# Gated-delta pairs: scaling inside the inversion, first solve ahead of the sixth output slot, outputs of both directions in one bank

## The reference, cut to what matters

```
u = rms_norm(h);  z = u @ w_in            # one input projection for all three groups
y = concat(rwkv7(z_rw), gated_delta(z_gd), mlstm(z_ml))
h = h + y @ w_out
h = h + (silu(gate) * val) @ w_down       # gate, val from conv(rms_norm(h) @ w_up)
h = h + sigmoid(rms_norm(h) @ w_ple_gate) * (p @ w_ple_proj)
```

```
L   = strict_lower((k * beta) @ k.T * decay)
u,w = solve(I + L, [v * beta, k * beta * exp(g)])
v_new = u - w @ S
o = (q * exp(g)) @ S + lower(q @ k.T * decay) @ v_new
S = S * exp(g_last) + (k * exp(g_last - g)).T @ v_new
```

## Time and profile before

| what | us |
|---|---|
| median of three runs | 3178.64 (3175.67 to 3181.02) |
| the profiled execution, its span | 3174.6 |
| PE busy in it | 3054.9 (96%) |
| DVE busy | 2081.5 (66%) |
| ACT busy | 1657.2 (52%) |
| POOL busy | 612.3 (19%) |

### The profile page before, as it was taken

One profiled execution on the slowest core, in us unless ns is written; L12 is line 12 of the kernel. 1 busy time (PEld: TensorE's weight loads), 2 busy tenths in 40 slices (PEclk: granted clock), 3 DMA queues, 4 the chain that ended last, 5 costly groups with the idle time before them and its releaser, 6 DMA issues.

```text
span 3174.6 us, 56293 instructions
## 1 busy us (share of the span) xinstructions
PE 3054.9 (96%) x20767; PEld 2626.2 (83%) x20767; DVE 2081.5 (66%) x3474; ACT 1657.2 (52%) x2673; POOL 612.3 (19%) x517
## 2 busy tenths in 40 slices
PE   8999988899999999999999999889899999999998
PEld 7899877777888888888788998777688888888886
DVE  6775655777777777455568655567767777774554
ACT  6555654456555555444455556545465555544444
POOL 2000453440212222000000005334402221220000
PEclk9999998999999999999999999999899999999999
DMA  6666101114656666666556660021256665666664
GB/s 208 185 180 187 47 2 59 61 55 146 195 185 192 192 182 196 221 195 191 164 169 194 183 178 15 2 66 55 67 178 193 184 192 181 196 198 215 193 183 152
DMA packets 265227, 479.22 MB, mean 151 GB/s; under 512 B 17314, under 2 KB 81148, under 8 KB 264380
## 3 DMA queue, kind: packets, MB, share of 16 engines
q1 hardware_dynamic: 265020, 476.48, 49.1%
HBM read 474.32 MB, written 2.10 MB: 150 GB/s over the span
## 4 chain that ended last, share of the span: by engine, by line
PE 87%; DVE 8%; ACT 1%; issue 1%; DVEq 1%; POOL 0%; SPq 0%; DMA 0%; ACTq 0%; POOLq 0%
PE ps L643 86%; PE ps L647 1%; DVE scores L2194 1%; DVE wlo L1801 1%; DVE XS L1851 0%; ACT L1272 0%; DVE upair L1814 0%; DVE TN L1860 0%; DVE AR L2221 0%; DVE H L1833 0%; ACT XS L1272 0%; DVE st L1875 0%; DVE TN L2246 0%; DVE heads L1880 0%; POOL H L580 0%
## 5 line engine op out<-in xcount | busy, mean ns | idle before, releaser
L1801 DVE TENSOR_TENSOR wlo<-ring,whi 128x1024 fp32r<-128x1024 f32 (+4 forms) x905 | 1095.6, 1229 | 672.2 <-ACT whi L1272 666.3
L643 PE MATMUL ps<-upair,whi 128*128 128x512 f32 x4032 | 1404.4, 394 | 6.3 <-DVE upair L1814 5.7
L1272 ACT ACTIVATE whi<-ring 128x1024 fp32r<-128x1024 f32 (+4 forms) x947 | 941.0, 1002 | 795.6 <-PE ps L643 715.8
L643 PE MATMUL ps<-upair,wlo 128*128 128x256 f32 x4032 | 1121.2, 278 | 0.0
L643 PEld LDWEIGHTS ps<-upair,whi 128*128 128x128 f32 x4032 | 756.5, 188 | 182.9 <-issue 6.1
L643 PEld LDWEIGHTS ps<-upair,wlo 128*128 128x128 f32 x4032 | 758.9, 188 | 0.3 <-issue 0.2
L643 PE MATMUL ps<-whi,upair 128*128 128x390 f32 (+2 forms) x1280 | 367.5, 364 | 0.0
L625 POOL TENSOR_TENSOR YB<-YB 128x1024 f32<-128x1024 f32 x22 | 125.3, 5697 | 828.9 <-DVE YB L1824 828.9
L643 PE MATMUL ps<-whi,ghi 128*128 128x512 f32 x704 | 274.4, 390 | 0.0
L643 PE MATMUL ps<-whi,glo 128*128 128x512 f32 x704 | 274.0, 389 | 0.0
L643 PE MATMUL ps<-wlo,ghi 128*128 128x512 f32 x704 | 273.9, 389 | 0.0
(11 more groups left out here) (311 smaller groups left out, 3621.5 us busy)
## 6 DMA issues: line engine op xcount, KB each, us to landing
ring<-in_w_up_dram SPq DMA_DIRECT2D x352, 512.0 KB, 3.9
ring<-in_w_down_dram SPq DMA_DIRECT2D x176, 512.0 KB, 4.3
ring<-in_w_in_dram SPq DMA_DIRECT2D x128, 384.0 KB, 3.5
ring<-in_w_out_dram SPq DMA_DIRECT2D x64, 512.0 KB, 3.7
ring<-in_w_ple_gate_dram SPq DMA_DIRECT2D x64, 512.0 KB, 4.4
ring<-in_w_in_dram SPq DMA_DIRECT2D x51, 512.0 KB, 4.5
ring<-in_w_in_dram SPq DMA_DIRECT2D x64, 390.0 KB, 3.5
ring<-in_w_in_dram SPq DMA_DIRECT2D x32, 396.0 KB, 3.6
```

Of the source, the lines that this page charges most:

```text
L643: return pe.matmul(o_, a, b, start=start, stop=stop, skip_group_check=True)
L1272: return act.activation(o_, i_, f, **kw)
L1801: v.tensor_tensor(wlo[:, slot % RING, :, 0:w], ring[:, slot % RING, :, 0:w], whi[:, slot % RING, :, 0:w].bitcast(F32), SUB).then_inc(S["lo ...
```

## The change

It has four parts, all in the pair loop.

1. The scaling of values and keys moves from behind the inversion into it: direction 0 behind the XS of level 2, direction 1 behind the XS of level 4 (a new hook `amid` in DVE's `invert`). It writes to other tiles: VS, in the place of sgate, and KW, in the place of zlora (the listing of instructions names it Z).
2. On PE the first solve follows the inversion at once. The sixth output slot, `out_slot(i, 5)`, is cut in halves: one stands behind the solve, one behind `gd_ks`. The mLSTM's fifth stage moves behind `gd_state`, and the attention products with the solution move behind the second half of the slot.
3. On ACT the copies of the second solve (KBt) move ahead of the table load, the mLSTM's inverse root and the third partial result, and the copy whi of the next pair's first slot moves between the two solves' copies. The solution goes to a tile of its own, `solved`.
4. On DVE the mLSTM's fifth stage moves behind the state copies, and the sum and squares of its heads behind rf and XS. The outputs of both directions are accumulated in one bank, ps[3], and DVE adds XS to them straight from PSUM, where before it copied ps[3], added ps[7] and then added XS.

```diff
@@ -248,8 +248,10 @@
 
         uf = [XS[d][:, 2:4, :] for d in range(2)]
         S0 = [XS[d][:, 0:2, :] for d in range(2)]
-        ufg = [scores[d][:, 0, 2:4, :] for d in range(2)]
-        S0g = [scores[d][:, 0, 0:2, :] for d in range(2)]
+        VS = [sgate[:, d, :].rearrange("p (u c) -> p u c", c=P) for d in range(2)]
+        KW = [zlora[:, d, :].rearrange("p (h c) -> p h c", c=P) for d in range(2)]
+        solved = at("solved", [P, 2, 4, P], u_place + 20480)
+        ufg, S0g = ([solved[:, d, 2 * i:2 * i + 2, :] for d in range(2)] for i in range(2))
         pT = XS[0][:, :, :].rearrange("p a c -> p (a c)").rearrange("p (k t) -> p k t", t=T)
 
         ps = [ctx.enter_context(nc.psum_tensor(f"ps{i}", [P, 512], F32)) for i in range(8)]
@@ -1062,20 +1064,22 @@
                             last = turn(ps[(1, 5)[t]][:, c * P:(c + 1) * P], YB[:, t, col:col + P])
                         last.then_inc(S["yt_psum"], 1)
 
-                def out_slot(g, s, banks=OUT_BANKS):
+                def out_slot(g, s, banks=OUT_BANKS, halves=range(NT)):
                     i, j = divmod(s, 2)
...
+                    for t in halves:
...
+                    if NT - 1 in halves:
+                        last.then_inc(S["slot_done"], 1)
 
                 def squared_sums(n, banks):
                     pe.wait_ge(S["gd_sq"], n + 1)
...
-                    invert(m2, lambda d, j: scores[d][:, 2, j, :], {lv: lambda lv=lv: ml_pair(n, n2, lv) for lv in (1, 2, 4, 5)},
+                    invert(m2, lambda d, j: scores[d][:, 2, j, :], {lv: lambda lv=lv: ml_pair(n, n2, lv) for lv in (1, 2, 4)},
...
-                    out_slot(i, 5)
                     for d in range(2):
                         F = FIRST[d]
                         inverted(m2, d)
                         pe.wait_ge(S["gd_rhs"], n2 + (d + 1))
                         for h in range(2):
-                            last = mm(ps[4 * d][:, h * P:(h + 1) * P], TT[d][:, 2 * h + F, :], TN[d][:, 2 * h + F, :], True, True)
+                            last = mm(ps[4 * d][:, h * P:(h + 1) * P], TT[d][:, 2 * h + F, :], VS[d][:, 2 * h + F, :], True, True)
                         last.then_inc(S["gd_u"], 1)
-                    pe.wait_ge(S["ml_numc"], n2 + 2)
+                    out_slot(i, 5, halves=(0,))
                     for d in range(2):
                         F = FIRST[d]
                         pe.wait_ge(S["gd_uf"], n2 + (d + 1))
                         for h in range(2):
-                            last = mm(ps[4 * d + 2][:, h * P:(h + 1) * P], XS[d][:, h, :], ufg[d][:, h, :], True, True)
+                            last = mm(ps[4 * d + 2][:, h * P:(h + 1) * P], KW[d][:, h, :], ufg[d][:, h, :], True, True)
                         last.then_inc(S["gd_state"], 1)
-                        for h in range(2):
-                            j = 2 * h + F
-                            mm(ps[4 * d + 3][:, j * P:(j + 1) * P], scores[d][:, 3, j, :], ufg[d][:, h, :], True, True)
+                    ml_pair(n, n2, LEV - 1)
                     for d in range(2):
                         B = 1 - FIRST[d]
                         pe.wait_ge(S["gd_s0"], n2 + (d + 1))
@@ -1163,6 +1164,13 @@
                                 last = mm(ps[4 * d + 2][:, (2 * j + h) * P:(2 * j + h + 1) * P], AR[h][:, B, j, :],
                                           S0g[d][:, h, :], True, True)
                         last.then_inc(S["gd_ks"], 1)
+                    out_slot(i, 5, halves=(1,))
+                    pe.wait_ge(S["ml_numc"], n2 + 2)
+                    for d in range(2):
+                        F = FIRST[d]
+                        for h in range(2):
+                            j = 2 * h + F
+                            mm(ps[3][:, j * P:(j + 1) * P], scores[d][:, 3, j, :], ufg[d][:, h, :], d == 0 and h == 0, False)
                     for d in range(2):
                         B = 1 - FIRST[d]
                         pe.wait_ge(S["gd_rs"], n2 + (d + 1))
@@ -1174,8 +1182,8 @@
                         pe.wait_ge(S["gd_usc"], n2 + (d + 1))
                         for h in range(2):
                             j = 2 * h + B
-                            last = mm(ps[4 * d + 3][:, j * P:(j + 1) * P], scores[d][:, 3, j, :], KBt[d][:, h, :], True, True)
-                        last.then_inc(S["gd_y"], 1)
+                            last = mm(ps[3][:, j * P:(j + 1) * P], scores[d][:, 3, j, :], KBt[d][:, h, :], False, True)
+                    last.then_inc(S["gd_y"], 1)
...
@@ -1644,16 +1652,16 @@
...
-                    split_out(sg, lg, 8)
                     for src, dst, lo, done in (("gd_u", ufg, 0, "gd_uf"), ("gd_us", KBt, T, "gd_usc")):
                         if src == "gd_us":
-                            partial_out(ng, sg, 2)
-                            ready_logs()
-                            act.wait_ge(S["ml_ss"], n + 1)
-                            rsqrt(st[:, 2, :], st[:, 1, :], 1.0 / P, epsb[:, 0:1]).then_inc(S["ml_rstd"], 1)
+                            split_out(sg, lg, 8)
                         for d in range(2):
                             act.wait_ge(S[src], n2 + (d + 1))
                             a(mono(dst[d][:, :, :], 2), ps[4 * d][:, lo:lo + T], ACT.Copy).then_inc(S[done], 1)
+                    ready_logs()
+                    act.wait_ge(S["ml_ss"], n + 1)
+                    rsqrt(st[:, 2, :], st[:, 1, :], 1.0 / P, epsb[:, 0:1]).then_inc(S["ml_rstd"], 1)
+                    partial_out(ng, sg, 2)
...
@@ -1840,7 +1848,7 @@
...
-            def invert(m2, between=None, before_last=None):
+            def invert(m2, between=None, before_last=None, amid=None):
                 ml = v.snap(m2 * LEV)
                 for lv in range(LEV):
                     for d in range(2):
@@ -1852,6 +1860,8 @@
                                 .then_inc(S["inv_xs"], 1)
                         else:
                             v.tensor_copy(mono(XSb[d][LATE[d], :, :]), ps[4 * d][LATE[d], 0:2 * P]).then_inc(S["inv_xs"], 1)
+                    if amid:
+                        amid(lv)
...
@@ -2234,34 +2244,39 @@
...
-                    invert(m2, lambda lv: lv and ml_pair(i, n, n2, lv), products)
-
-                    v.wait_ge(S["gd_vtc"], n + 1)
-                    v.wait_ge(S["gd_ktc"], n + 1)
-                    for d in range(2):
+                    def scaled(lv):
+                        if lv not in (2, LEV - 2):
+                            return
+                        d = 0 if lv == 2 else 1
                         F = FIRST[d]
-                        v.wait_ge(S["inv_t"], m2 * LEV + (2 * LEV - 1 + d))
+                        if d == 0:
+                            v.wait_ge(S["gd_vtc"], n + 1)
+                            v.wait_ge(S["gd_ktc"], n + 1)
                         for h in range(2):
                             for t in range(NT):
-                                v.tensor_scalar(TN[d][:, 2 * h + t, :], Vt[:, 2 * h + t, :], gs[:, 20 + 2 * t + d, h:h + 1], None, MUL)
-                            v.tensor_scalar(XS[d][:, h, :], OT[:, 2 * h + F, :], gs[:, 16 + 2 * F + d, h:h + 1], None, MUL)
+                                v.tensor_scalar(VS[d][:, 2 * h + t, :], Vt[:, 2 * h + t, :], gs[:, 20 + 2 * t + d, h:h + 1], None, MUL)
+                            v.tensor_scalar(KW[d][:, h, :], OT[:, 2 * h + F, :], gs[:, 16 + 2 * F + d, h:h + 1], None, MUL)
                         v.scalar_tensor_tensor(gs[:, 4 + d:8 + d:2, :], gs[:, 20 + d:24:2, :], -1.0, gs[:, 12 + d:16:2, :], MUL, MUL)\
                             .then_inc(S["gd_rhs"], 1)
-                    v.drain()
-                    v.tensor_tensor(OL, OL, msq, ADD)
-                    head_squares("ml", msq)
+
+                    invert(m2, lambda lv: lv and lv < LEV - 1 and ml_pair(i, n, n2, lv), products, scaled)
+
                     for d in range(2):
                         v.wait_ge(S["gd_state"], n2 + (d + 1))
                         v.tensor_copy(mono(S0g[d], 2), ps[4 * d + 2][:, 0:T]).then_inc(S["gd_s0"], 1)
+                    ml_pair(i, n, n2, LEV - 1)
                     for d in range(2):
                         B = 1 - FIRST[d]
                         v.wait_ge(S["gd_ks"], n2 + (d + 1))
                         for h in range(2):
                             v.scalar_tensor_tensor(rf[d][:, h, :], ps[4 * d + 2][:, h * P:(h + 1) * P], gs[:, 4 + 2 * B + d, h:h + 1],
-                                                   TN[d][:, 2 * h + B, :], MUL, ADD)
+                                                   VS[d][:, 2 * h + B, :], MUL, ADD)
                             last = v.tensor_scalar(XS[d][:, 2 + h, :], ps[4 * d + 2][:, (2 + h) * P:(3 + h) * P],
                                                    gs[:, 12 + 2 * B + d, h:h + 1], None, MUL)
                         last.then_inc(S["gd_rs"], 1)
+                    v.drain()
+                    v.tensor_tensor(OL, OL, msq, ADD)
+                    head_squares("ml", msq)
...
```

(15 more changed lines are left out.)

13 lines of the change are left out of this document (6 added, 7 removed).

## The result

| | median us | runs |
|---|---|---|
| before | 3179.0 (3175.67 to 3181.02) | 4 |
| changed | 3200.82 (3199.5 to 3209.55) | 4 |

The ratio is 1.0068, 95% interval 1.0046 to 1.0089: slower, by 21.8 us at the medians. Run once more on another chip, the changed kernel gave a median of 3196.36 in seven runs beside 3179.33, ratio 1.0056 (1.0036 to 1.0076). The profiled execution has a span of 3197.8 us, 23.2 above that of before.

The account below looks back on a forecast made before the run. TensorE, busy 96% of the span, was taken as the bound. -1.5 + 0.4 + 6.6 + 6.0 + 1.6 = +13.1 us on 3174.6 gave 3187.7; with 4.0 for the median of the runs, 3191.7, range 3178 to 3203.

Parts of the forecast that it names:

- Part 1, the solve on PE: End of each pair on PE: four waits around the solves go, 2.7 us per pair if nothing else came last.
- Part 2, ACT's order: End of a layer's first two pairs: squared sums wait for ACT's third partial, PE idle 3.7 us; -1.5 us in all.
- The hand-over: From a pair's end to the next pair, DVE last: YB ready 0.4 us earlier in each of four places.
- The third pairs: End of each layer's third pair, through DVE's mLSTM sums and ACT's rstd: +0.2 us each, +0.4 in all.
- Part 3, the hold: Inversion level 2, second and third pairs: POOL holds DVE's SBUF scalings, PE starts 1.65 us later; +6.6 us in four places.
- Rival A: Scalings pass beside POOL undisturbed, so 6.6 and 1.6 fall away: +4.9 us, 3183.5; chance 0.16.
- Part 4, the clock: Low granted clock behind PE's new idle times: +6.0 us at the squared sums, +1.6 at level 2, four places each.
- Rival B: Scalings are held, but the clock stays up after the new idle times: +5.5 us, 3184.1; chance 0.15.
- Rival C: Shorter wait for YB keeps the clock up there, with scalings undisturbed and the idle harmless: -7.7 us, 3170.9; chance 0.09.
- The direct additions: DVE adding both directions straight from PSUM, without the ps[3] copy: costed at nothing beyond the instruction-by-instruction replay.
- the replay: The new order of the pair loop replayed instruction by instruction with the durations of the kernel before.
- rival D: All on the dear side, scalings held 2.5 us, 3.3 and 1.4 us of clock: +27.7 us, 3206; chance 0.12.

Follow-up runs that it names:

- e8: The changed kernel with 30 unused transpositions on PE where it waits for the third partial result; 3184.8 us beside 3179.3 for the kernel before.
- e7: The kernel before with only the scalings of both directions moved inside the inversion; 3179.3 us beside 3179.3 for the kernel before.
- e2: The changed kernel with ACT copying the third partial result ahead of the two copies into KBt; 3185.1 us beside 3187.9 for the kernel before.
- e6: The changed kernel run again unaltered; 3196.4 us beside 3179.3 for the kernel before.
- e11: The kernel before with only both directions' outputs in one bank and DVE's two direct additions from PSUM; 3171.8 us beside 3186.2 for the kernel before.

## Why the prediction was right, and where it was not

- **Part 1, the solve on PE: right.** The last products of KBt were to end at 567.1 and end at 566.7.
- **Part 2, ACT's order: right.** The partial was to be out at 570.7, PE idle for 3.7 us; measured 570.06 and 3.42. The hand-over was put at -0.4 a place without the clock: e8 has -0.72. The sentence that what is won on PE ahead of that copy changes nothing holds for the changed kernel only. With ACT's order of before the same waits are worth 1.6 us in each of six pairs (e7), and with the partial early an end of the changed kernel is 2.4 us shorter (e2). So the new order on ACT cost more than the delay that I counted: it also hid the gain.
- **The third pairs: right.** +0.2 each, measured +0.26 and -0.04. But e7 shows that there, too, 1.6 us could be had, and the change gave them away; which of its parts did was not run singly.
- **Part 3, the hold: right in kind, with both terms mis-sized.** PE's products at level 3 were to start at 614.4 and start at 614.67, but YB's transposes come 0.66 later too. Counted from them, the products are late by 1.12 to 1.48 us in the four places, 1.33 in the mean, not 1.65. From there to the last TT copy another 1.0 us is lost in each place, where 0.4 was forecast. Together that is 2.33 against 2.05. The wait of 3.14 us is not itself the price: with the low clock no longer ahead of it (605.30), PE comes to the wait 1.9 us earlier, and it pays for the low clock behind it. The prediction took that stretch for a new one; it is one that moved. In e6 it stayed ahead in two of the places; there PE waits 1.5 us and the middle is 1.4 us longer. Rival A fell; the row nearer to the case was indeed the copy from SBUF, not the scaling from PSUM. Of the two held rows that the prediction names, only L2131 is a copy; L2221 combines two tiles.
- **Part 4, the clock: right at the squared sums.** 1.5 a place was forecast there, 1.67 by e8. Rival B fell. Rival C's premise fell as well: the wait for YB is down to 1.95 us, and the clock is at 0.50 from 588.00 to 594.60 all the same.
- **The direct additions: in the replay, without a term of their own.** I gave them nothing beyond the replay, as DVE waits afterwards. That reason is wrong: alone they shorten every end by 1.33 us (e11), because DVE's reduction decides when POOL starts, and POOL decides how long DVE is held later. The 1.3 us that the replay won at L2221 is of that size, and in e8 the way from the squared sums to YB's transposes is 15.73 us instead of 17.05. A run of the changed kernel without them was not made.
- **The sum: the step that failed.** -1.5 + 0.4 + 6.6 + 6.0 + 1.6 = +13.1 (four places of -0.4 are -1.6, a slip of 0.1), and the pairs measured +13.3. In the same terms the runs give -2.9 + 0.2 + 5.3 + 6.7 + 4.0, so the agreement to 0.2 us is luck: the errors cancel. The error of 9.1 us lies outside the pairs: I took the rest of the program as equal in both kernels, and in the execution profiled, the up projection of layer 0 ran at its slower rate, +9.0 us. Nothing in the one trace of before could show that, as both its layers had the faster rate. The median of 3200.8 lies above the 3186 to 3198 that the forecast itself claimed. It is inside the range only because that was left wide for rival D, which did not happen; this is luck as well.

## What to carry to other kernels

Before work moves into an engine's idle gap, look at what the other engines do in that gap: a gap of 3.1 us on DVE was no room for 1.3 us of scalings while POOL was running, but the gap on ACT was. When waits are removed from one engine, follow the order of the next one down to the last instruction that someone waits for; here a copy of 1.06 us, set behind two table loads, took all that the solve had won. Compare stages, not totals: the pair stages of the changed order stood at 13.3, 13.4 and 11.1 us in three traces, while the totals jumped by 9 for a cause outside them.

## What the runs showed of the hardware

- PE's uninterrupted stream in the up projection runs at one of two rates, with no idle time and a granted clock of 1.00 at both: from the start of a 512-column product to the next start 231.7 or 236.3 ns, for 256 columns 115.0 or 117.0 (means over a loop; three loops at the faster rate have 230.0 and 116.7, the same sum). In the opening blocks of the stage the stream has two breaks of 314 to 319 ns, behind gaps of some 1490 and 480 ns. At the second the rate changed from one to the other in all 28 layers of the 14 traces, at the first in 9 of them; in the kernel before it stayed at the first break in both layers, in the changed kernel's first trace it changed there in layer 0. What decides at the first break is open.
- A granted clock of 0.50 stood behind each of the two new waits of PE (3.42 and 3.14 us), and work of no use in the first of them took it away (e8). But a wait is not always ahead of it: the kernel before has 0.50 at 605.30, where PE had not waited since 588.96. Where the low clock falls moves with the waits ahead of it, so the price of a wait can't be read from the wait alone.
- DVE operations that read and write SBUF were held to the end of POOL's instruction one after the other, with one of them let through at each change (608.33 to 613.5). No semaphore stands between the two, so engines do not wait for each other through semaphores only. The same scalings on ACT, at the same time, were not held, nor were those on DVE in the first pair, where POOL was idle.
